# Two transformer blocks on one core: attention steps re-ordered and shared out anew, tail in two halves

## The reference

```python
qa = apply_rope(rms_norm(qa, q_norm_a), ang_axial)   # 8 heads of 64, keys and values 2 heads
s = einsum(q, k) * scale; p = softmax(s); o = einsum(p, v)            # group A, all 512 keys
qb, kb = apply_rope(qb, ang_1d), apply_rope(kb, ang_1d)               # group B
s = where(|qpos - kpos| <= 128, s, -inf); softmax with a sink term    # group B, 256 or 384 keys
...
gate = sigmoid(rms_norm_2(x, norm_ple) @ w_ple_gate)
x = x + gate * (p @ w_ple_proj)
out = rms_norm_2(x, norm_final)
```

## Time and profile before

| | us |
|---|---|
| median of 3 runs (lowest, highest) | 1373.84 (1373.65, 1375.49) |
| the profiled execution | 1378.3 |
| its span | 1376.5 |
| TensorE busy | 1329.5 (97%) |
| VectorE busy | 694.8 (50%) |
| ScalarE busy | 546.1 (40%) |
| GpSimd busy | 150.3 (11%) |

### The profile page before, as it was taken

How to read it: one execution, slowest core, us unless ns; L and a number is a source line. 1 busy time by engine, 2 the same in 40 slices (tenths; PEclk the granted TensorE clock), 3 DMA queues, 4 the chain that set the end, 5 groups by cost and what they waited for, 6 DMA issues and landing times.

```text
span 1376.5 us, 14683 instructions
## 1 busy us (share of the span) xinstructions
PE 1329.5 (97%) x6056; PEld 1066.9 (78%) x6056; DVE 694.8 (50%) x907; ACT 546.1 (40%) x733; POOL 150.3 (11%) x136
## 2 busy tenths in 40 slices
PE   7987989999999999999999999999999999999995
PEld 5764657888888888887888777888888888888874
DVE  6998773665444442126534455563544354423254
ACT  6558864543233222225224555542423232222232
POOL 3351012510000000103000001012000000010021
PEclk9999989999999999999999999999999999999997
DMA  6110003122222222331321111233222223232311
GB/s 242 62 61 1 1 1 122 63 92 95 106 105 92 92 75 94 105 96 66 130 92 62 62 62 64 90 99 115 94 92 92 92 94 107 69 105 92 117 62 61
DMA packets 20594, 117.74 MB, mean 86 GB/s; under 512 B 2480, under 2 KB 2864, under 8 KB 9904
## 3 DMA queue, kind: packets, MB, share of 16 engines
q1 hardware_dynamic: 19680, 114.79, 23.8%
q10 hardware_dynamic: 848, 2.01, 0.4%
HBM read 114.70 MB, written 2.10 MB: 85 GB/s over the span
## 4 chain that ended last, share of the span: by engine, by line
PE 89%; DVE 7%; DMA 1%; ACT 1%; issue 1%; SPq 0%; POOLq 0%; POOL 0%; DVEq 0%
PE ps L474 87%; PE ps L675 2%; DVE rt L1264 1%; DVE w_lo L1257 1%; DMA w_raw<-weights 1%; DVE nmax L1430 1%; DVE F L1261 1%; DVE rt L1257 0%; DVE hf L1257 0%; DVE OUT L1264 0%; DVE h_lo L1264 0%; ACT w_hi L862 0%; DVE y L1257 0%; DVE y L1264 0%; DVE diag L1261 0%
## 5 line engine op out<-in xcount | busy, mean ns | idle before, releaser
L474 PE MATMUL ps<-h_hi,w_hi 128*128 128x512 f32 x1248 | 495.2, 397 | 13.2 <-DVE w_lo L1257 10.6
L474 PE MATMUL ps<-h_lo,w_hi 128*128 128x512 f32 x1248 | 487.4, 391 | 0.0
L474 PE MATMUL ps<-h_hi,w_lo 128*128 128x512 f32 x1248 | 487.2, 390 | 0.0
L1257 DVE TENSOR_TENSOR w_lo<-w_raw,w_hi 128x2048 fp32r<-128x2048 f32 (+2 forms) x117 | 246.4, 2109 | 266.8 <-ACT w_hi L862 266.8
L474 PEld LDWEIGHTS ps<-h_hi,w_hi 128*128 128x128 f32 x1248 | 235.2, 188 | 69.7 <-issue 13.8
L862 ACT ACTIVATE w_hi<-w_raw 128x2048 fp32r<-128x2048 f32 (+2 forms) x117 | 201.1, 1721 | 191.0 <-DMA w_raw<-weights 190.8
L474 PEld LDWEIGHTS ps<-h_lo,w_hi 128*128 128x128 f32 x1248 | 235.3, 189 | 51.0 <-issue 3.1
L474 PEld LDWEIGHTS ps<-h_hi,w_lo 128*128 128x128 f32 x1248 | 235.1, 188 | 49.7
L418 POOL TENSOR_TENSOR sqsum<-sqsum,sq 128x512 f32<-128x512 f32 x66 | 95.6, 1448 | 917.5 <-ACT sq L862 915.9
L474 PE MATMUL ps<-mid_hi,w_hi 128*128 128x512 f32 x352 | 136.9, 389 | 0.0
L474 PE MATMUL ps<-mid_lo,w_hi 128*128 128x512 f32 x352 | 136.9, 389 | 0.0
(11 more groups left out here) (187 smaller groups left out, 1188.0 us busy)
## 6 DMA issues: line engine op xcount, KB each, us to landing
w_raw<-weights SPq DMA_DIRECT2D x81, 1024.0 KB, 4.8
w_raw<-weights SPq DMA_DIRECT2D x32, 704.0 KB, 3.9
out_t<-OUT SPq DMA_DIRECT2D x8, 256.0 KB, 2.0
X<-x_t SPq DMA_DIRECT2D x3, 512.0 KB, 7.4
c<-constants ACTq DMA_DIRECT2D x1, 1280.0 KB, 8.8
w_raw<-weights SPq DMA_DIRECT2D x4, 256.0 KB, 8.4
wp_raw<-weights SPq DMA_DIRECT2D x1, 1024.0 KB, 7.0
X<-x_t SPq DMA_DIRECT2D x2, 256.0 KB, 4.1
```

The costliest lines, as they stand in the source:

```text
L474: return nc.tensor.matmul(out, lhsT, rhs, start=start, stop=stop, skip_group_check=loose)
L1257: return nc.vector.tensor_tensor(out, a, b, op)
```

## The change

- q and k are stored with the high parts of two heads on all 128 partitions (`QA[:, 0, c]`) and the low parts beside them. The scores of a pair of heads, same query block, are six matmuls of 64 rows, alternating between the lower and the upper half of the partitions (hi*hi, hi*lo, lo*hi). Steps come in such pairs; there are four score banks and four row buffers instead of three.
- In steps 0 to 31 GpSimd multiplies the row by the reciprocal, and VectorE copies the transposed block of every odd step (behind its reciprocal three steps later); ScalarE copies the others. In steps 32 to 63 VectorE scales and ScalarE copies, as before.
- The low parts of q and k are made by VectorE. Chunks are evacuated into eight buffers in `PP`, without waiting for earlier ones.
- Roping of chunk 8 moves from the projection to step 33, chunks 9 and 10 to 36 and 39, the second value chunk to 28; the weight split of step 17 goes to 43, and unit 6's split comes right before the steps.
- The weighted sums of a pair of heads wait for the copy of the pair before, in one bank; only the last pair has another.
- Tail: the last gate chunk and everything behind it go by halves of 256 tokens, with six stores in place of eight, one issued by ScalarE. The running sum on TensorE doesn't wait for the last chunk.

The diff, cut to what the text speaks of:

```diff
-LATE1 = 9
+LATE1 = 8
+LATE_STEP = {11: 28, 8: 32, 9: 35, 10: 38}
...
-    (1, h, b, max(b - 1, 0), min(b + 2, NB)) for h in range(NH) for b in range(NB)]
+STEPS = [(0, 2 * c + n, b, 0, NB) for c in range(NH // 2) for b in range(NB) for n in range(2)] + [
+    (1, 2 * c + n, b, max(b - 1, 0), min(b + 2, NB)) for c in range(NH // 2) for b in range(NB) for n in range(2)]
 
...
-        prob, rt_late = F[:, 4:7, :], F[:, 0:2, :]
+        prob, rt_late = F[:, 4:8, :], F[:, 0:2, :]
...
-            return y[:, j % 3, :] if j < LATE1 else y_late[j - LATE1]
+            return PP[:, j, :] if j < KD else y_last[j - KD]
...
+        def copied_by_dve(s):
+            return s < HALFWAY and s % 2 == 1
+
+        def copied(s):
+            if copied_by_dve(s):
+                return pt_dve, s // 2 + 1
+            return pt_ready, s // 2 + 1 if s < HALFWAY else HALFWAY // 2 + s - HALFWAY + 1
+
+        def tr_bank(s):
+            return 4 + (s + 1) % 2
+
+        def out_bank(c):
+            return 6 if c < 7 else 5
...
+        STORES = [(0, 0, 4), (0, 4, 8), (1, 0, 3), (1, 3, 5), (1, 5, 7), (1, 7, 8)]
...
-            for j in range(len(ORDER1)):
-                if ORDER1[j] not in V1:
-                    low_qk(j)
+            for s in range(HALFWAY):
+                pool.wait_ge(rden_ready, s + 1)
+                if s:
+                    pool.wait_ge(pn_pool, s)
+                nc.gpsimd.tensor_scalar(prob[:, s % 4, :], prob[:, s % 4, :], rden[:, s:s + 1], None, ALU.mult
+                                        ).then_inc(pn_pool, 1)
...
-                for part in range(2):
-                    last = mm(ps[:, bank, at:at + w], q[:, h, b * P:(b + 1) * P], k[:, part, h // 4, k0 * P:k1 * P],
-                              part == 0, kind == 0 and part == 1, loose=kind == 1)
+                    pe.wait_ge(sink_ready, 2 * (t - 16) + 2)
+                for qp, kp in ((0, 0), (0, 1), (1, 0)):
+                    for n in range(2):
+                        r = slice(HD * n, HD * n + HD)
+                        last = mm(ps[:, (2 * t + n) % 4, at:at + w], q[r, qp, c, b * P:(b + 1) * P],
+                                  k[r, kp, (c // 2 + n) % 2, k0 * P:k1 * P], (qp, kp) == (0, 0),
+                                  kind == 0 and qp == 1, loose=True)
...
-                    if c >= 2:
-                        pe.wait_ge(ot_ready, c - 1)
-                    pe.wait_ge(pt_ready, 8 * (c + 1))
+                    if c:
+                        pe.wait_ge(ot_ready, c)
+                    else:
+                        pe.wait_ge(hvar_ready, len(NORMED))
+                    pe.wait_ge(*copied(8 * c + 6))
+                    pe.wait_ge(*copied(8 * c + 7))
...
-            scores(1)
             for s, (kind, h, b, k0, k1) in enumerate(STEPS):
-                scores(s + 2)
+                if s % 2 == 0:
+                    scores(s // 2 + 1)
                 if s >= 10 and s % 2 == 0:
                     weighted((s - 10) // 8, (s - 10) % 8 // 2)
-                if s in LATE_STEPS:
-                    item(LATE_STEPS[s])
-                pe.wait_ge(pn_ready, s + 1)
-                if s == 0:
-                    free_item(LATE1 - 2)
-                if s == 1:
-                    free_item(LATE1 - 1)
+                for j, at in LATE_STEP.items():
+                    if s == at:
+                        item(j)
+                if s < HALFWAY:
+                    pe.wait_ge(pn_pool, s + 1)
+                else:
+                    pe.wait_ge(pn_ready, s - HALFWAY + 1)
+                if s < 2:
+                    free_item(LATE1 - 1 - s)
                 if s >= 2:
-                    pe.wait_ge(pt_ready, s - 1)
+                    pe.wait_ge(*copied(s - 2))
...
+            sums, square = sqsum[:, :], sq[:, 1, :]
+            pe.wait_ge(*n_final.summed(KD))
+            final_part(0, sums)
+            final_part(1, sums)
+            for i in range(2):
+                pe.wait_ge(*n_final.squares(KD + i))
+                final_part(i, square).then_inc(n_final.total.sem, 1)
+            final_factor(0)
+            final_factor(1)
...
-                if 3 <= j < LATE1:
-                    if ORDER1[j - 3] in V1:
-                        act.wait_ge(v_ready, V1.index(ORDER1[j - 3]) + 1)
-                    else:
-                        act.wait_ge(rope_done, roped_upto(j - 3))
-                if j == LATE1:
+                if j == 9:
...
+                if copied_by_dve(s):
+                    return
...
-                if s >= 3:
-                    act.wait_ge(tr_done, s - 2)
+                if s >= 4:
+                    act.wait_ge(tr_done, s - 3)
                 at = SINK_AT + 1 - w if kind else 0
-                af(prob[:, s % 3, 0:w], ps[:, s % 3, at:at + w], ACT.Exp, bias=nmax[:, s:s + 1],
+                af(prob[:, s % 4, 0:w], ps[:, s % 4, at:at + w], ACT.Exp, bias=nmax[:, s:s + 1],
                    accum_out=den[:, s:s + 1]).then_inc(exp_done, 1)
                 if s >= 2:
                     copy_pt(s - 2)
-                if s % 8 == 2 and s > 10:
-                    copy_out((s - 18) // 8)
-                if s in (5, 9):
-                    high_qk(9 if s == 5 else 10)
-                if s == 12:
-                    finish(11)
-                if s == 16:
+                if s % 8 == 1 and s > 10:
+                    copy_out((s - 17) // 8)
+                for j, at in LATE_STEP.items():
+                    if s == at + 2:
+                        finish(j)
+                        high_qk(j)
+                if s == 42:
...
             square_group(n_group_b, 4, 0)
+            copy_out(6)
             square_group(n_group_b, 4, 1)
-            copy_out(6)
...
+            half_gate(0)
+            half_square(0)
+            half_gate(1)
             tables(LN_EXP)
-            guess(n_final)
+            half_square(1)
+            half_guess(0)
+            half_guess(1)
...
+                low_qk(j - 1)
+            low_qk(LATE1 - 1)
+            split(UNITS_IN1)
...
+            def copy_pt(s):
+                kind, h, b, k0, k1 = STEPS[s]
+                dve.wait_ge(tr_done, s + 1)
+                if s >= 16 and s % 8 == 1:
+                    dve.wait_ge(av_done, s // 8 - 1)
+                nc.vector.tensor_copy(PT_slots[h % 4][:, k0:k1, b * P:(b + 1) * P],
+                                      ps[:, tr_bank(s), :].rearrange("p (b c) -> p b c", b=NB)).then_inc(pt_dve, 1)
...
+                if s < HALFWAY:
+                    nc.vector.reciprocal(rden[:, s:s + 1], den[:, s:s + 1]).then_inc(rden_ready, 1)
+                else:
+                    link(nc.vector.reciprocal(rden[:, s:s + 1], den[:, s:s + 1]))
+                    ts(prob[:, s % 4, 0:w], prob[:, s % 4, 0:w], rden[:, s:s + 1], ALU.mult).then_inc(pn_ready, 1)
+                if s >= 3 and copied_by_dve(s - 3):
+                    copy_pt(s - 3)
                 negmax(s + 2)
-                if s in (3, 7):
-                    rope(9 if s == 3 else 10)
-                if s == 17:
+                for j, at in LATE_STEP.items():
+                    if s == at + 1:
+                        rope(j)
+                    if s == at + 3:
+                        low_qk(j)
+                if s == 43:
...
+            for i in range(2):
+                half_gate_in(i)
+                half_gate_out(i)
+            half_variance(0)
+            half_variance(1)
+            half_factors(0)
+            half_factors(1)
+            half_apply(0, 0, KD)
+            half_apply(1, 0, KD)
```

More of the change, by code:

```diff
@@ L554, in _ @@
             KS = range(KD)
-            LATE_STEPS = {1: 9, 5: 10, 9: 11}
             def free_item(j):
@@ L640, in scores @@
+                if kind:
+                    for n in range(2):
+                        bank = (2 * t + n) % 4
+                        if b:
+                            last = mm(ps[:, bank, at:at + P], ident_r[:, :], mask_r[:, 0, :], False, True, loose=True)
+                        if b + 1 < NB:
+                            last = mm(ps[:, bank, at + w - P:at + w], ident_r[:, :], mask_r[:, 1, :], False, True,
+                                      loose=True)
                 last.then_inc(s_done, 1)
@@ new lines, in half_factors, with half_apply @@
+            def half_factors(i):
+                b = slice(2 * i, 2 * i + 2)
+                dve.wait_ge(*n_final.guess(i + 1))
+                link(refine(stat[:, 3, b], stat[:, 0, b], stat[:, 2, b]))
+                for c in (2 * i, 2 * i + 1):
+                    last = ts(diag[:, c, :], ident[:, :], stat[:, 3, c:c + 1], ALU.mult)
+                last.then_inc(n_final.diag.sem, 1)
+            def half_apply(i, k0, k1):
+                dve.wait_ge(*n_final.factor(i + 1))
+                for k in range(k0, k1):
+                    stt(OUT[:, k, half_of(i)], X[:, k, half_of(i)], gcol("norm_final_2", k),
+                        ps[:, FACTOR_BANKS[i], 0:HALF], ALU.mult, ALU.mult).then_inc(out_ready, 1)
```

230 lines of the change are left out of this document (132 added, 98 removed).

## The result

| | before | after |
|---|---|---|
| median (lowest, highest), us | 1374.66 (1373.65, 1378.61), 4 runs | 1409.67 (1407.56, 1410.66), 4 runs |
| ratio, 95% interval | | 1.0237 (1.0224 to 1.0250): slower |
| the profiled execution, its span | 1378.3, 1376.5 | 1410.66, 1408.9 |
| maximum 0 starts | 99.77 | 95.26 |
| maximum 0 to maximum 32 | 54.12 | 73.15 |

The forecast was 1378.7 in a range up to 1386.0. The direction was right, the size was not: +4.9 us was forecast for the profiled execution, and +32.4 was found (+35.0 between the medians, since the profiled execution of before lies at the upper end of its runs). The parts of the difference: projection -4.5, first 32 steps +19.0, last 32 steps +21.7, end of attention +0.8, tail -4.7; together 32.3. The maxima are the row maxima on VectorE, one for each attention step, so their distance is the time of the steps between them.

What follows compares the result with a forecast made beforehand. TensorE was taken to bound the kernel (89% of the span), with VectorE nearly full in attention. -4.0 + 5.9 + 8.0 + 1.0 - 6.0 = +4.9 us, added to the median 1373.84, gave 1378.7; range 1368.0 to 1386.0.

Steps and rivals of the forecast that it cites:

- Projection: Before step 0: TensorE's waits for GpSimd and rope end and chunk 8's rotation leaves, 4.0 us earlier.
- Row halves at once: Attention scores: matmuls on the two row halves run together, six in three waves taking 0.91 us.
- GpSimd's multiply: First 32 steps: one-input 128x512 multiply taken as 0.9 us, between bounds 0.44 and 1.45; up to 1.5 hides.
- The loop of the first half: First 32 steps: a new loop through VectorE's copy of odd blocks takes 3.9 us a pair where 2.97 was.
- The sum of the first half: First 32 steps: 14 pairs of 3.9 us plus 5.4 fill, 60.0 against 54.1, so 5.9 us later.
- the clock as a rival: First half: waits in the new loop halve TensorE's clock, 6.5 us over five pairs, 1385.2; chance 0.08.
- The last 32 steps: Steps 32 to 63: late chunks and mode changes make them 8.0 us later than 53.3 us.
- The late chunks and the split: Last 32 steps: 9.7 us of added VectorE work, partly in idle time, costs 7.5 us; bounds nothing and 9.7.
- Mode changes and the new form of the scores: Last 32 steps: one score product in four saved, but two more mode changes per pair, +0.5 us.
- The late chunks fall into VectorE's idle time: Last 32 steps, rival: 13.3 us idle absorbs 9.7 of late work; sum -3.1, 1370.7 us; chance 0.28.
- End of attention: Last pair's weighted sums wait for ScalarE's copy of the pair before, 1.0 us later on TensorE's path.
- Tail: After the last gate chunk: working by halves makes the end 6.0 us earlier, bounds 4.5 and 7.5.

Runs made afterwards that it cites:

- e12: e9 with the first head group's rows multiplied by the constant 1/512 in place of VectorE's reciprocal; 1378.7 us.
- e2: Changed kernel with VectorE copying each odd transposed block one step earlier, two steps later instead of three; 1401.6 us.
- e9: Changed kernel with the scores of the next pair one step earlier on TensorE, ahead of the transposes; 1383.6 us.
- e4: Changed kernel with VectorE scaling and ScalarE copying again in steps 0 to 31; 1381.3 us, ratio 1.0032 to before.
- e7: Changed kernel with four unused matmuls added on TensorE ahead of its wait in odd steps from 2 to 25; 1406.5 us.
- e5: Changed kernel with the late chunks at steps 4, 8, 12 and 16 and the weight split at 20; 1404.3 us.
- e6: e4 with the late chunks at steps 4, 8, 12 and 16 and the weight split at 20; 1372.3 us, ratio 0.9967 to before.

## Why the prediction was right or wrong, step by step

**Projection: right.** 4.0 us earlier forecast, 4.5 found, and no wait over 0.5 us is left on TensorE between 38 and 95 us. Maximum 0 itself moves by some 1.2 us between traces of the same code. The subtractions of a k chunk with its copies took 2.09 us ("about 2"), and between 38 and 95 us VectorE's two-input operations of 128x512 took 0.68 to 0.74 us, not 1.74 as in the earlier trace rows.

**Row halves at once: right.** Six score matmuls take 0.96 us, 0.91 forecast.

**GpSimd's multiply: wrong in size.** 0.9 taken, 1.57 measured, and the upper bound of 1.45 was under it as well. The step that failed is "since it reads half of what the upper one reads": with a constant it takes 1.49 us (e12) and the two-input addition 1.30, so half the reading doesn't halve the time. The Trainium skill, "GPSIMD Engine Reference", section 3, gives 769 ns for 512 elements as the best case of a loop; that is half of what this instruction took here, and the trace decides. By itself this error was small, as I had said, since 1.5 us would hide: two multiplies in the fill, 1.3 us, and part of the 0.17 a pair.

**The loop of the first half: half right, and near by luck.** I forecast 3.9 us a pair through VectorE's copy and 4.07 was found, but at the limit was another loop, which I had overlooked: the reciprocal of an odd step stands behind the next maximum. With my 0.9 us for the multiply it would by estimate have been 3.4 us and not have counted; with 1.57 it overtakes the copy by 0.13. No run has the copy's loop alone at the limit; the 0.13 puts it at 3.94 by estimate. e2 (no gain without the copy loop), e9 (3.46 without both) and e4 (2.93 with the old sharing) show this.

**The sum of the first half: wrong, 5.9 forecast, 19.0 found.** Working from the rows: the fill up to maximum 4 took 7.9 us, 5.4 forecast (+2.5: two multiplies 1.3, and transposes and scores at the lower clock 1.1). Loop 4.07 for 3.9 in 14 pairs: +2.4. Clock: +6.0 (e7). The remaining 2.2 are two pairs in which ScalarE also copies a finished pair of heads, and the last one before maximum 32 (4.78, 4.77 and 4.94 us in e7). I had the clock as a rival at 0.08, and priced it well (6.5 us), but as a case *in place* of the forecast. It isn't: a pair of 3.9 us bound by other engines is itself what leaves TensorE idle. Not every such loop pays it, though: in e9, with pairs of 3.46 bound by GpSimd, the mean clock of the first half was 0.97. The chance was wrong, and so was treating it as exclusive.

**The last 32 steps: wrong, 8.0 forecast, 21.7 found.** The late chunks and the split: 7.5 forecast, 13.0 found (e5; 12.7 by e6). My upper bound was their own 9.7 us of VectorE time, and it was no bound, because behind each rope maxima, scores and transposes are late one after the other (in e4 TensorE stands four times for VectorE's scaling between 156 and 173 us, 5.3 us together, and e6 has none of these waits) and the clock is lower (0.67 from 173 to 193 us in e4). How the extra 3.3 us divide between the two no run shows. Mode changes and the new form of the scores: 0.5 forecast, 1.2 found (e6 against before: a remainder, and smaller than what two traces of the same code differ by). And 7.5 us where the halves meet (e5 against e6, 6.3 of them found at that place in the traces, as are 7.7 between the changed kernel and e4), which weren't in the sum at all: I had written "the new loop is not here", but its last two copies are. Together 13.0 + 1.2 + 7.5 = 21.7; they add up by construction, as the differences from kernel to kernel along after, e5, e6 and before.

**"The late chunks fall into VectorE's idle time" (0.28): refuted** by e5, with more idle time than before on VectorE, 7.8 us were still paid in the first half.

**End of attention: right.** 1.0 forecast, 0.8 found; the wait for ScalarE's copy stands in the row of 245.15.

**Tail: right in kind, 6.0 forecast, 4.7 to 5.0 found.** Moved by the 37.1 us by which it starts later, the last chunk was ready at 1356.9 (1356.5 forecast; the addition of the row of 1392.69 ends 0.5 us behind TensorE's last matmul) and the outputs began at 1362.7 (1362.4 forecast). A half output took 0.40 and not 0.36 us (+0.6 on sixteen), and the last store ended 2.8 us behind the last output, not 2.4.

**What made it wrong as a whole.** Each of my mechanisms existed. But in the sum every part had its price at full clock and every wait its own length, and the range took the rivals as alternatives. Here they came together, and in the first half they fed one another: loop, idle TensorE, lower clock, longer loop (e7). Each by itself would have left the time in the range or 0.2 us beyond its end: 6.0 for the clock, 5.5 more for the late chunks, 7.5 where the halves meet.

## What to carry to other kernels

Write the loop of a hand-ordered pipeline for every engine's list, not for one: follow each operation to the one that stands *ahead* of it in its own list, whether they have to do with one another or not. When work leaves a full engine, ask first whether the order can be changed (moving six matmuls ahead of four transposes was worth 26 us here, with GpSimd's slow multiply still in place). And where a change makes TensorE wait, add the price of the lower clock to the sum, not to the rivals; late work that is inserted into such a loop can cost more than its own duration (1.3 times it in the second half, 0.7 times in the first).

## What the runs showed of the hardware

- A one-input fp32 multiply of 128x512 on GpSimd takes 1.56 us with a factor by partition and 1.49 with a constant, more than its two-input addition in the same kernel (1.30 in the median, 1.47 in the mean).
- The granted clock fell from 1.00 to 0.50 in e6 behind sixteen one-column matmuls (rows below: 175 to 177 us, then 179 to 181), though the profile has TensorE busy without a gap. So a stretch that the profile shows as busy throughout can be followed by the lower clock. What made it fall no run settles.

```profile
175.00:177.00 2.00, 2.00 (x18) 1.54 (x17) 1.51 (x5) 1.04 (x3) 0.00 (x0) 1.00 0.00 0
177.00:179.00 2.00, 2.00 (x17) 1.75 (x16) 0.73 (x4) 1.17 (x6) 0.53 (x1) 0.82 0.00 0
179.00:181.00 2.00, 2.00 (x10) 1.22 (x8) 0.49 (x2) 0.47 (x3) 0.00 (x0) 0.50 0.07 16
```

- VectorE's addition of 128x256 took 1.40 us beside GpSimd's sum (the row of 1392.69) and 0.42 without it (1395.37 in the same trace).
